# Four sums of weight pieces per pair of blocks, moved from VectorE to adding transfers of POOL's queue

## The reference

```
x = x + mixed @ w_out[l]                                          # 2048 x 2048
h2 = rmsnorm(x, norm_ffn[l])
x = x + jnp.square(jax.nn.relu(h2 @ w_up[l])) @ w_down[l]         # 2048 x 8192, 8192 x 2048
```

## Time and profile before

| | |
|---|---|
| median of 3 runs | 2548.11 us |
| lowest, highest | 2547.83, 2558.79 us |
| span of the profiled execution | 2548.7 us |
| feed-forward stretch (17 pairs, two blocks) | from about 1755 us to the end |
| PE, DVE, ACT, POOL busy over the span | 98%, 74%, 55%, 17% |
| TensorE clock granted | 0.996 of 2.4 GHz in the mean |

### The profile page before, as it was taken

The page is one execution under the profiler, slowest core; times in us unless marked ns, Lnnn a source line. Parts: engine busy times, 40 slices in busy tenths (PEclk is TensorE's granted clock), DMA queues, the critical chain, the costliest instruction groups (busy, mean ns, idle before and its releaser), DMA issues.

```text
span 2548.7 us, 32976 instructions
## 1 busy us (share of the span) xinstructions
PE 2498.2 (98%) x11898; PEld 2064.7 (81%) x11898; DVE 1889.3 (74%) x2807; ACT 1408.5 (55%) x1956; POOL 431.7 (17%) x288
## 2 busy tenths in 40 slices
PE   5999999999999999998999999999999999999999
PEld 4888888888887888887887777888888888888887
DVE  7899887866677777766655555557887878888884
ACT  4555764444447555556476666655565545545553
POOL 0155563111021000010000000024111111111111
PEclk9999999999999999999999999999999999999999
DMA  9989777878784867654545455454656464656454
GB/s 346 329 288 346 241 252 275 318 279 287 255 285 153 241 204 208 198 182 149 182 149 174 155 165 165 149 182 149 218 176 219 163 231 166 218 177 212 169 203 160
DMA packets 355131, 549.11 MB, mean 215 GB/s; under 512 B 32332, under 2 KB 126128, under 8 KB 354608
## 3 DMA queue, kind: packets, MB, share of 16 engines
q1 hardware_dynamic: 353168, 541.24, 62.9%
q10 hardware_dynamic: 1824, 6.04, 0.6%
HBM read 545.13 MB, written 2.10 MB: 215 GB/s over the span
## 4 chain that ended last, share of the span: by engine, by line
PE 89%; DVE 5%; issue 3%; ACT 2%; DMA 1%; SPq 0%; DVEq 0%; ACTq 0%; POOL 0%; POOLq 0%
PE ps L2193 48%; PE ps L2198 24%; PE ps L2223 2%; PE ps L2219 2%; PE ps L2220 2%; DVE ps L1220 1%; PE ps L2178 1%; DVE lo L1191 1%; PE ps L2180 1%; PE ps L2179 1%; PE ps L2272 1%; ACT hi L533 1%; PE ps L2562 1%; DVE lo L1167 1%; PE ps L2795 1%
## 5 line engine op out<-in xcount | busy, mean ns | idle before, releaser
L1191 DVE TENSOR_TENSOR lo<-raw,hi 128x1024 fp32r<-128x1024 f32 x550 | 716.4, 1318 | 394.8 <-ACT hi L533 394.2
L533 ACT ACTIVATE hi<-raw 128x1024 fp32r<-128x1024 f32 x550 | 576.0, 1058 | 457.8 <-PE ps L2198 361.8
L2193 PE MATMUL ps<-hi,a_hi 128*128 128x512 f32 (+1 forms) x2016 | 800.5, 397 | 1.2 <-DVE a_lo L1402 0.9
L2193 PE MATMUL ps<-hi,a_lo 128*128 128x512 f32 (+1 forms) x2016 | 786.2, 390 | 0.0
L2198 PE MATMUL ps<-lo,a_hi 128*128 128x512 f32 (+1 forms) x2016 | 539.0, 389 | 0.0
L520 ACT ACTIVATE hi<-raw 128x1024 fp32r<-128x1024 f32 x339 | 358.2, 1060 | 293.1 <-PE ps L2198 255.8
L1167 DVE TENSOR_TENSOR lo<-raw,hi 128x1024 fp32r<-128x1024 f32 x339 | 424.5, 1271 | 106.5 <-ACT hi L520 104.4
L2193 PEld LDWEIGHTS ps<-hi,a_hi 128*128 128x128 f32 x2016 | 379.1, 188 | 81.9 <-issue 3.2
L2198 PEld LDWEIGHTS ps<-lo,a_hi 128*128 128x128 f32 x2016 | 378.4, 188 | 79.6
L2193 PEld LDWEIGHTS ps<-hi,a_lo 128*128 128x128 f32 x2016 | 379.2, 188 | 74.2
L2193 PE MATMUL ps<-hi,b_hi 128*128 128x512 f32 x880 | 348.0, 395 | 0.6 <-ACT hi L520 0.3
(11 more groups left out here) (339 smaller groups left out, 2616.1 us busy)
## 6 DMA issues: line engine op xcount, KB each, us to landing
raw<-in_ada_w SPq DMA_DIRECT2D x96, 1024.0 KB
raw<-in_sgu_w_in SPq DMA_DIRECT2D x96, 1024.0 KB
raw<-in_w_up SPq DMA_DIRECT2D x64, 1024.0 KB
raw<-in_w_down SPq DMA_DIRECT2D x64, 1024.0 KB
raw<-in_w_in SPq DMA_DIRECT2D x42, 1024.0 KB
raw<-in_sgu_w_out SPq DMA_DIRECT2D x32, 1024.0 KB
raw<-in_w_in SPq DMA_DIRECT2D x128, 256.0 KB
raw<-in_mla_w_in SPq DMA_DIRECT2D x33, 512.0 KB
```

The source lines that it names most:

```text
L533: nc.scalar.activation(hi[:, q % CHUNKS, :], raw[:, r % RAWS, q % 2 * CW:(q % 2 + 1) * CW], ACT.Copy).then_inc(hi_ready, 1)
L1191: nc.vector.tensor_tensor(lo[:, q % CHUNKS, :], raw[:, r % RAWS, q % 2 * CW:(q % 2 + 1) * CW], hi[:, q % CHUNKS, :].bitcast(F32), ALU.subt ...
L2193: nc.tensor.matmul(ps[:, 2 * s + t, 0:width], x[:, k0 + j, t * P:(t + 1) * P], hi[:, c, w], start=begins, stop=False)
```

## The change

The four sums leave DVE. POOL issues four transfers per pair that read a piece of `raw`, or the new buffer `both`, and add it to their target in the chip's memory (`accum_op=ALU.add`), 512 KB each. W11 + W21 gets a home of its own, `both`, 4 KB per partition: SP loads W11 into it a second time, right behind slab `a`, and a transfer adds W21. Item 6 is read from there. The other sums change places in slab `a`: item 4 and item 12 now stand where W12 stood. Slab `b` is needed until item 12, so its home is freed with that of `a`, two at once (before: `b` after item 10). The order in which slabs find homes shifts with it.

```diff
-PAIR_CHUNKS = (("a", 1), ("p", 0), ("a", 0), ("p", 1), ("a", 0), ("p", 2), ("a", 1), ("p", 3), ("b", 1), ("p", 4), ("b", 0), ("p", 5), ("a", 0),
+PAIR_CHUNKS = (("a", 1), ("p", 0), ("a", 0), ("p", 1), ("a", 1), ("p", 2), ("e", 0), ("p", 3), ("b", 1), ("p", 4), ("b", 0), ("p", 5), ("a", 1),
...
-        last = {s: max(i for i, name in enumerate(names) if name == s) for s in slabs}
+        last = {s: W_ALL if s == "b" else max(i for i, name in enumerate(names) if name == s) for s in slabs}
...
                 sp.dma_start(to(raw[:, slot, :]), source).then_inc(landed[slot], LAND)
+                if s == "a":
+                    if pair:
+                        sp.wait_ge(lo_ready, chunk_of(pair - 1, W11_21) + 1)
+                    sp.dma_start(both[:, :].rearrange("p (k n) -> p k n", k=2), source[:, :, 0:NB]).then_inc(both_landed, 16)
+                    pair += 1
...
-            act.wait_ge(landed[place.slot], place.landed)
-            if place.item in (2, 4, 6, 12):
-                act.wait_ge(w_mixed, 4 * place.pair + (2, 4, 6, 12).index(place.item) + 1)
+            if place.item in (W11_12, W11_12_21, W11_21, W_ALL):
+                act.wait_ge(weights_added[place.item], 16 * (place.pair + 1))
+            else:
+                act.wait_ge(landed[place.slot], place.landed)
...
+        def add_first(pool, pair):
...
+            a, b, w11, w12, w21, w22 = weight_pieces(pair)
+            a, b, w11, w12, w21, w22 = weight_pieces(pair)
+            pool.wait_ge(landed[a.slot], a.landed)
+            pool.dma_start(w11, w12, accum_op=ALU.add).then_inc(weights_added[W11_12], 16)
...
+        def add_second(pool, pair):
...
+            a, b, w11, w12, w21, w22 = weight_pieces(pair)
+            pool.wait_ge(both_landed, 16 * (pair + 1))
+            pool.wait_ge(landed[b.slot], b.landed)
+            pool.dma_start(by_rows(both[:, :]), w21, accum_op=ALU.add).then_inc(weights_added[W11_21], 16)
...
+        def add_third(pool, pair):
...
+            a, b, w11, w12, w21, w22 = weight_pieces(pair)
+            pool.wait_ge(weights_added[W11_12], 16 * (pair + 1))
+            pool.wait_ge(weights_added[W11_21], 16 * (pair + 1))
+            pool.wait_ge(lo_ready, chunk_of(pair, W12) + 1)
+            pool.dma_start(w12, by_rows(both[:, :]), accum_op=ALU.add).then_inc(weights_added[W11_12_21], 16)
...
+        def add_last(pool, pair):
...
+            a, b, w11, w12, w21, w22 = weight_pieces(pair)
+            pool.wait_ge(lo_ready, chunk_of(pair, W11_12_21) + 1)
+            pool.dma_start(w12, w22, accum_op=ALU.add).then_inc(weights_added[W_ALL], 16)
...
+            def summed_pair(pair, first, second):
+                add_last(pool, pair)
+                first()
+                if pair + 1 < pairs:
+                    add_first(pool, pair + 1)
+                    add_second(pool, pair + 1)
+                    add_third(pool, pair + 1)
+                second()
```

More of the change, by code:

```diff
@@ L204, in ffn_plan @@
         for i, ((s, k), name) in enumerate(zip(chunks, names)):
-            mixed = s in "ab"
-            places[FFN_CHUNK + len(places)] = Place(slot[name], landed[name], k if mixed else None, None if mixed else k % 2,
-                                                    last[name] == i, pairs, None if kind == "last" else i)
+            mixed, own = s in "ab", s == "e"
+            places[FFN_CHUNK + len(places)] = Place(None if own else slot[name], None if own else landed[name], k if mixed else None,
+                                                    k % 2 if not (mixed or own) else None,
+                                                    sum(at == i for at in last.values()), pairs, None if kind == "last" else i)
         freed += len(slabs)
@@ L213, with chunk_of @@
 FFN_LOADS, FFN_PLACES = ffn_plan()
+def chunk_of(pair, item):
+    return next(q for q, place in FFN_PLACES.items() if (place.pair, place.item) == (pair, item))
 def build(nc, d, out):
@@ L252, in build @@
         raw = sb("raw", [P, RAWS, 2 * CW])
+        both = sb("both", [P, CW])
         stage = sb("stage", [P, T, NB])
@@ L342, in build @@
         lb_ready = sem("lb_ready")
[L343 to L344 removed]
+        weights_added = {item: sem(f"weights_added{item}") for item in (W11_12, W11_12_21, W11_21, W_ALL)}
+        both_landed = sem("both_landed")
+        x_mixed, x_mixed_hi, x_mixed_lo, p1_kept, up_relu = (
+            sem(k) for k in ("x_mixed", "x_mixed_hi", "x_mixed_lo", "p1_kept", "up_relu"))
         block = ctx.enter_context(nc.Block())
@@ L480, in _ @@
             w_out2, w_up, w_down = d["w_out_2"][0], d["w_up_2"][0], d["w_down_2"][0]
+            pair = 0
             for slot, free, kind, c, b, s in FFN_LOADS:
@@ L503, in raw_piece @@
         def raw_piece(place):
+            if place.slot is None:
+                return by_rows(both[:, :])
             s = raw[:, place.slot, :]
@@ L1160, in lo_planned @@
             place = FFN_PLACES[q]
[L1161 to L1165, removed]
             dve.wait_ge(hi_ready, q + 1)
@@ L1168, in lo_planned @@
                                     ALU.subtract).then_inc(lo_ready, 1)
[L1169 to L1180, removed]
             if place.frees:
-                nc.vector.memset(tick[:, place.slot:place.slot + 1], 0.0).then_inc(raw_free, 1)
+                nc.vector.memset(tick[:, place.slot:place.slot + 1], 0.0).then_inc(raw_free, place.frees)
         def lo_next(dve, n, ahead=AHEAD):
@@ L2039, in pool_take, with weight_pieces @@
             n.acc.base += 2
+        def weight_pieces(pair):
+            first = chunk_of(pair, W12)
+            piece = lambda item, half: raw_piece(FFN_PLACES[first + item]._replace(half=half))
+            return FFN_PLACES[first + W12], FFN_PLACES[first + W22], *(piece(i, h) for i in (W12, W22) for h in range(2))
+        def add_first(pool, pair):
[17 more added lines that the diff above has]
+            pool.dma_start(w12, w22, accum_op=ALU.add).then_inc(weights_added[W_ALL], 16)
         def pool_pairs(pool, n, n_turns, op):
@@ L2170, in _ @@
-            for b in range(3):
-                pool_take(pool, n, lambda t: add_x(t, lambda base: slice(b * NB, (b + 1) * NB)))
+            pairs = FFN_PLACES[max(FFN_PLACES)].pair
+            def summed_pair(pair, first, second):
[6 more added lines that the diff above has]
+                second()
@@ new lines, in down, with up, squares @@
+            def down(pair, p):
+                at = lambda second: lambda base: slice(base + (2 * p + second) * NB, base + (2 * p + second + 1) * NB)
+                summed_pair(pair, *(lambda second=second: pool_take(pool, n, lambda t: add_x(t, at(second))) for second in range(2)))
+            def up(pair, c, p):
+                def squares(second):
+                    b = 2 * p + second
+                    for t in range(T):
+                        pool.wait_ge(up_relu, 8 * c + 2 * b + t + 1)
+                        one = v[:, t, c % 2 * D + b * NB:c % 2 * D + (b + 1) * NB]
+                        tt(one, one, one, ALU.mult).then_inc(stage_free, 1)
+                    n.stg.base += 2
+                    n.acc.base += 2
+                summed_pair(pair, lambda: squares(0), lambda: squares(1))
@@ L2174, in three @@
+            for pair, (kind, c, b) in enumerate(unit for unit in FFN_UNITS if unit[0] != "last"):
+                if kind == "up":
+                    up(pair, c, b)
+                else:
+                    down(pair, b)
+            pool_take(pool, n, lambda t: add_x(t, lambda base: slice(2 * NB, 3 * NB)))
         def three(out_, x_hi, x_lo, w_hi, w_lo, start, stop, weights_first=False):
```

19 lines of the change are left out of this document (6 added, 13 removed).

## The result

| | before | changed |
|---|---|---|
| median, lowest to highest (us) | 2549.53, 2547.83 to 2558.79 (4 runs) | 2656.18, 2647.88 to 2657.44 (4 runs) |
| ratio of changed to before | | 1.0409, 95% interval 1.0392 to 1.0426 |
| profiled execution: time, span | 2548.7 (span) | 2655.82, 2653.8 |
| TensorE clock granted, mean share | 0.996 | 0.981 |

The account below looks back on a forecast made before the run. PE's own pace bounds the kernel, DVE isn't waited for. Profiled span 2548.7 - 1.0 for PE's waits + 0.9 for new waits in pair 0 = 2548.6; less 0.6, median 2548.0 us; range 2545 to 2612.

Parts of the forecast that it names:

- the chain to item 4: Before item 4 of each pair: three POOL transfers in series, the third landing at 2073.8, T + 5.5, costing PE nothing.
- T + 6.7: Latest landing of item 4's sum before PE waits, 2075.0; T is when PE starts the pair's item 0, 2068.30.
- the fixed 2.0: Fixed part of each POOL transfer's time: 2.0 us, between bounds of 1.7 and 3.4.
- the work of an adding transfer: Moving part of a 512 KB adding transfer: 2.6 us for two reads, between bounds of 1.3 and 3.9.
- slab `b` is in at T - 5.0: Landing of slab `b` with the change, put at 2063.3, after which the second transfer was to start.
- the fourth transfer and the later slabs are covered: Fourth transfer needs 5 to 8 us of its 15; q1, 2.6 us later, is still in time: nothing on the path.
- Sharing the engines with it costs `b` half of its work, 1.3 us: Slab `b` shares the DMA engines with the first transfer, adding 1.3 us to `b`'s landing.
- The DMA engines are idle from 2066 to 2075 now, so it shares with nothing: The third transfer runs alone, taking 2.0 + 2.6 us and landing at 2073.8.
- The margin: Third transfer lands 1.2 us ahead of 2075.0; from 5.2 us per transfer PE waits, 17 times.
- Rival B: Adding transfers cost more than two reads; PE waits before item 4 of every pair, 2.1 us each: 2584; chance 0.28.
- Rival C: DVE holds up POOL's preparing of transfers, 1.2 us late per pair over 17 pairs: 2568; chance 0.10.
- D: A late slab or fourth transfer, from homes that free later, about 1 us per pair: 2565; chance 0.05.

## Why the prediction was wrong

Right were: that VectorE is not the bound, so that nothing is to be won but 1.1 us; that the chain to item 4 decides; its deadline of T + 6.7, near enough (item 4 keeps its length with the third in at T + 5.5, is up to 0.7 us longer with T + 6.4 to T + 7.0, and PE's list has a wait from T + 7.3 on); the fixed 2.0 and, near enough, the work of an adding transfer (2.9, not 2.6), 4.8 us alone for the forecast 4.6; that slab `b` is in at T - 5.0 (with more room the second, which needs it, started at that time); that the fourth transfer and the later slabs are covered (item 4 made free: 0.16% in all).

The sum failed in **The chain for item 4**, step by step:

1. "Sharing the engines with it costs `b` half of its work, 1.3 us". That was the charge to `b`; the other side, what the slabs do to the first transfer, was left out. It takes 8.4 us in this pair and lands at T - 1.5. The second was taken to start when `b` is in, T - 5.0. It starts at T - 1.2. With more room it started at T - 5.0 and took 6.7 in the median, 7.9 in that pair. The step that failed is the start of the second: the sum had it wait for `b` and `both` only, and it waited for the first transfer to land, in all 17 pairs. With more room that wait goes, but the 1.3 us of sharing does not cover a link that is issued into engines with slabs still to do. 2 to 4 us were to be charged, on either account.
2. "The DMA engines are idle from 2066 to 2075 now, so it shares with nothing". They were idle because VectorE's sum of line 1178 stood ahead of the memset that lets p2 go; that sum ended at 2074.78, T + 6.5. The change takes the sum away, the order of the instructions in front of me showed it, and p2 goes at T + 3.2, ahead of the third. The window that I counted on was made by the very work that was removed, and the packets show the third waiting behind p2 until 2171. Holding p2 back gave 41 us with POOL's four transfers, 47 us with three.
3. The sum with these. The second starts 3.8 us later; from its issue to that of the third are 5.4 us where I had 5.9 (-0.5); the third takes 7.0 for 4.6 (+2.4). So it lands 5.7 us later, at T + 11.2 for T + 5.5. The margin was 1.2 by my deadline; PE's list has a wait of 4.0 in this pair, as it counts up to `hi` and not up to `lo`. The 16 waits make 67.5.
4. The clock. No term stood for it, and no row of before could show one, as PE never paused there. The granted clock's mean gives an estimate of its size from above: 2653.8 x 0.019 - 2548.7 x 0.004 = 40.2 us, and PE's rows grew by 36.0.

Rival B named the right place and wait, and was given 2584 for it. Its price came from 3.9 us of work per transfer; the work is 2.9, and what the sum lacked was the wait for the first to land and the company of the slabs. Cheaper transfers would have hidden that, as the copies show. Rival C, POOL held up by VectorE, falls: POOL's rows for preparing a transfer are 1.18 to 1.23 us beside VectorE or without it (one of the 68 takes 1.33). By the Trainium skill (SBUF — State Buffer, Who interferes with whom), a tensor_tensor doesn't keep POOL from writing descriptors; the trace agrees. D falls by the run with item 4 free. VectorE's busy time in 1950 to 2450 went from 422 to 373.91 with pairs of the old length, 48 us less where I had said 70. In that window the four lines of sums had 64.0 us (11 pairs, not 12), and the rows of `lo` grew by 8.4 us; the rest is open.

What stays open: by which rule a DMA engine chooses between the loads' queue and POOL's. In the pair shown POOL's packets came behind those of the slab issued first, and slabs issued earlier held an adding transfer up by 2 to 5 us. Open is also how the loss divides between the dearer adding, the room and the slabs before T; only p2's part (41 us) and the first transfer's (some 49 us with p2 held) were taken out one by one.

## What to carry to other kernels

Before counting on idle transfer engines, ask what keeps them idle: if it is the work that the change removes, the next load moves into the gap and meets the new transfers. A transfer on a path is priced with the loads issued ahead of it, not by itself; a chain of them multiplies this. Work moved off an engine that nobody waits for should go only where its result has slack. A gap on TensorE, when it sets the pace, can cost more than its length: here each gap of 3.2 us and more before item 4 was followed by half clock, most of those under 2 us were not. A list of waits can miss the short ones: so compare the length of the item too.

## What the runs showed of the hardware

- An adding transfer within the chip's memory keeps the DMA engines busy 2.2 times as long as a copy (88 and 40 us of one engine per MB), and takes 4.8 us for 512 KB when little else runs (3.2 as a copy); POOL spends 1.2 us on preparing it (0.72 for a copy).
- With the smaller room, POOL started the next adding transfer of 512 KB 0.3 us after the one before had landed (17 of 17 pairs, second at T - 1.2); with twice the room it did not wait for that (T - 5.0).
- The packets of POOL's third transfer, prepared by 2169.62, ran from 2171 on, behind those of slab p2, issued at 2167.35. With p2 held back it took 4.8 us in place of 6.9.
- After 4 us without a matmul PE ran at half clock for about three; keeping it busy with 92.6 us of useless matmuls cost 3.7 us in all. After waits of 1.2 us (pair 9) and of up to 1.7 us (VectorE's first sum, p2 held) the clock stayed full.
